# Attention units of two layers: the order of mixed probabilities and maxima on VectorE, two first convolution taps on ScalarE, two taps moved

## The reference

```python
p = jax.nn.softmax(sc, axis=-1)              # causal scores of both components of a head
a = p[:, :, 0] - lam * p[:, :, 1]            # mixed probabilities
o = jnp.einsum('bhqk,bhkv->bhqv', a, vt)
...
u = ga * jax.nn.sigmoid(gb)
u = causal_depthwise_conv(u, dw_conv_w[l], dw_conv_b[l])   # 31 taps and a bias for each channel
u = jax.nn.silu(layer_norm(u, conv_ln_g[l], conv_ln_b[l]))
```

## Time and profile before

| | |
|---|---|
| median of 3 runs | 1059.52 us (1059.42 to 1060.04) |
| profiled execution: time, span | 1060.15 us, 1058.0 us |
| TensorE busy | 1027.0 us (97%) |
| VectorE busy | 831.6 us (79%) |
| ScalarE busy | 525.1 us (50%) |
| attention units, layer 0 | about 396 to 447 us of the span |
| attention units, layer 1 | about 758 to 810 us of the span |

### The profile page before, as it was taken

The page is one execution under the profiler, slowest core; times in us unless marked ns, Lnnn a source line. Parts: engine busy times, 40 slices in busy tenths (PEclk is TensorE's granted clock), DMA queues, the critical chain, the costliest instruction groups (busy, mean ns, idle before and its releaser), DMA issues.

```text
span 1058.0 us, 19244 instructions
## 1 busy us (share of the span) xinstructions
PE 1027.0 (97%) x8174; PEld 983.7 (93%) x8174; DVE 831.6 (79%) x1117; ACT 525.1 (50%) x625; POOL 29.7 (3%) x54
## 2 busy tenths in 40 slices
PE   7999899999999999999999999999999999999998
PEld 6788899999998988989999999999888899999998
DVE  5889599998875999977988886879999676555552
ACT  5564665554435535545544343464455455444441
POOL 5100000000000010000000000000000000000000
PEclk9999999999999999999999999999999999999998
DMA  8576249799892654348599998846442475666551
GB/s 278 176 242 233 103 180 320 275 321 331 315 338 76 201 170 158 120 161 307 190 365 317 323 331 297 289 136 221 142 158 80 155 243 186 193 188 194 178 180 40
DMA packets 137473, 230.37 MB, mean 218 GB/s; under 512 B 7107, under 2 KB 60715, under 8 KB 137389
## 3 DMA queue, kind: packets, MB, share of 16 engines
q1 hardware_dynamic: 135060, 227.05, 62.8%
q10 hardware_dynamic: 921, 1.32, 0.5%
q0 software_dynamic: 1408, 0.79, 0.5%
HBM read 227.29 MB, written 1.06 MB: 216 GB/s over the span
## 4 chain that ended last, share of the span: by engine, by line
PE 69%; DVE 22%; ACT 6%; issue 2%; DMA 1%; SPq 0%; DVEq 0%; ACTq 0%
PE mm L437 66%; DVE lo L1313 7%; DVE cacc L1403 6%; ACT hi L852 1%; DVE ada_acc L1329 1%; DVE sB L1419 1%; DVE qk L1438 1%; DMA swap<-qk 1%; DVE hf L1436 1%; DVE qk L1437 1%; DMA raw<-in_w_in_dram 1%; DVE pB L1848 0%; DVE sA L1419 0%; ACT pB L931 0%; PE pa L544 0%
## 5 line engine op out<-in xcount | busy, mean ns | idle before, releaser
L437 PE MATMUL mm<-act_hi,hi 128*128 128x256 f32 x1760 | 487.7, 281 | 4.4 <-ACT act_hi L920 2.3
L437 PE MATMUL mm<-act_hi,lo 128*128 128x256 f32 x1760 | 483.0, 278 | 0.0
L437 PE MATMUL mm<-act_lo,hi 128*128 128x256 f32 x1760 | 466.0, 278 | 0.0
L1313 DVE TENSOR_TENSOR lo<-raw,hi 128x2048 fp32r<-128x2048 f32 (+1 forms) x159 | 359.5, 2264 | 117.8 <-ACT hi L852 114.8
L852 ACT ACTIVATE hi<-raw 128x2048 fp32r<-128x2048 f32 (+1 forms) x159 | 300.4, 1893 | 227.6 <-PE mm L437 172.7
L437 PEld LDWEIGHTS mm<-act_hi,hi 128*128 128x128 f32 x1760 | 332.2, 189 | 10.4 <-issue 7.2
L437 PEld LDWEIGHTS mm<-act_hi,lo 128*128 128x128 f32 x1760 | 333.5, 189 | 0.3
L437 PEld LDWEIGHTS mm<-act_lo,hi 128*128 128x128 f32 x1760 | 321.3, 189 | 0.0
L437 PE MATMUL mm<-u_hi,hi 128*128 128x256 f32 x608 | 169.3, 278 | 0.0
L437 PE MATMUL mm<-u_lo,hi 128*128 128x256 f32 x608 | 168.7, 278 | 0.0
L437 PE MATMUL mm<-u_hi,lo 128*128 128x256 f32 x608 | 168.7, 277 | 0.0
(11 more groups left out here) (285 smaller groups left out, 880.7 us busy)
## 6 DMA issues: line engine op xcount, KB each, us to landing
ada_raw<-in_ada_w_dram SPq DMA_DIRECT2D x128, 384.0 KB, 5.2
raw<-in_w_ffn_in_dram SPq DMA_DIRECT2D x88, 512.0 KB, 5.2
raw<-in_w_in_dram SPq DMA_DIRECT2D x39, 1024.0 KB, 5.1
raw<-in_w_ffn_out_dram SPq DMA_DIRECT2D x20, 1024.0 KB, 6.0
raw<-in_w_up_dram SPq DMA_DIRECT2D x16, 1024.0 KB, 6.5
raw<-in_w_down_dram SPq DMA_DIRECT2D x16, 1024.0 KB, 7.5
raw<-in_w_out_dram SPq DMA_DIRECT2D x12, 1024.0 KB, 5.9
raw<-in_w_in_dram SPq DMA_DIRECT2D x16, 512.0 KB, 6.2
```

Source lines behind the costliest of these rows:

```text
L437: ins = pe.matmul(o, w[:, kk, fs], a[:, k, :], start=(k == 0 and i == 0 and f % 2 == 0), stop=(ends and i == len(pairs) - 1), skip_group_c ...
L1313: v(dve.tensor_tensor(lo[:, c % RING, 0:nk, :], raw[:, c % RING, 0:nk, :], hi[:, c % RING, 0:nk, :].bitcast(F32), ALU.subtract), "lo_done")
```

## The change

- In units 0, 2 and 4 `probs2(i + 1)` (with the wait for its exponentials) is called ahead of `softmax_max(i + 2)` and `softmax_max(i + 3)`; the odd units 1, 3 and 5 don't call it any more. Unit 7 does as before.
- The first taps of channel tiles 2 and 3 are made by ScalarE: two activations (Identity, with the tap's weight as scale and the bias) on 128x256, ahead of the hi splits of group 2's stage, once VectorE has released `second_gated`. VectorE's generator leaves them out, hands out 122 taps, and waits for `second_begun` at that place.
- Two taps move: `TAPS_AT_IN[6]` goes from 7 to 5, `TAPS_AHEAD[1]` from 0 to 2.

```diff
@@ -41,8 +41,8 @@
 FAR = 3e38
 FAR_EXP = 41.0
 
-TAPS_AT_IN = (5, 8, 8, 8, 8, 0, 7, 1)
-TAPS_AHEAD = (5, 0, 5, 0, 5, 0, 8, 6)
+TAPS_AT_IN = (5, 8, 8, 8, 8, 0, 5, 1)
+TAPS_AHEAD = (5, 2, 5, 0, 5, 0, 8, 6)
 TAPS_BEHIND = (2, 9, 2, 9, 2, 9, 1, 0)
 UNITS = 8
 TAPS = 31
@@ -1153,6 +1153,10 @@
                 for g in (0, 1):
                     steps((l, "in", g))
                     evacuate((l, "in", g), qk2[:, 4 * g:4 * g + 4, :])
+                wait("second_gated")
+                for k in (2, 3):
+                    a(act.activation(cacc[:, k, :], cu[:, k, 0:S], ACT.Identity, scale=convw[:, GT * l + k, 0:1],
+                                     bias=pcols(("convb", l))[:, k:k + 1]), "second_begun")
                 steps((l, "in", 2))
                 evacuate((l, "in", 2), v2[:, :, :])
 
@@ -1396,10 +1400,15 @@
                     w = convw[:, GT * l + k, j:j + 1]
                     src = cu[:, k, j:j + S]
                     name = "conv_done" if j == TAPS - 1 else f"conv_step{k}"
+                    if j == 0 and k == 2:
+                        wait("second_begun", 2)
+                    if j == 0 and k >= 2:
+                        continue
                     if j == 0:
                         v(dve.tensor_scalar(cacc[:, k, :], src, w, pcols(("convb", l))[:, k:k + 1], ALU.mult, ALU.add), name)
                     else:
-                        dve.wait_ge(sem(f"conv_step{k}"), v.n.seen(f"conv_step{k}"))
+                        if j > 1 or k < 2:
+                            dve.wait_ge(sem(f"conv_step{k}"), v.n.seen(f"conv_step{k}"))
                         v(dve.scalar_tensor_tensor(out=cacc[:, k, :], in0=src, scalar=w, in1=cacc[:, k, :], op0=ALU.mult, op1=ALU.add), name)
                     yield
 
@@ -1813,7 +1822,7 @@
                     dve.wait_ge(sem(name), value)
                     k = slice(2 * part, 2 * part + 2)
                     u = cu[:, k, TAPS - 1:]
-                    link(dve.scalar_tensor_tensor(out=u, in0=csq[:, k, :], scalar=1.0, in1=u, op0=ALU.add, op1=ALU.mult))
+                    link(dve.scalar_tensor_tensor(out=u, in0=csq[:, k, :], scalar=1.0, in1=u, op0=ALU.add, op1=ALU.mult), "second_gated" if part else None)
 
                 def taps(count):
                     for _ in range(count):
@@ -1870,11 +1879,13 @@
                 for i in range(UNITS):
                     name, j = todoB(l)[i]
                     taps(TAPS_AHEAD[i])
-                    probs2(i)
+                    if i % 2 == 0 or i + 1 == UNITS:
+                        probs2(i)
                     advance(groups[name][1][j])
                     if i % 2 == 0 and i + 2 < UNITS:
+                        wait("exp_done", 2)
+                        probs2(i + 1)
                         softmax_max(i + 2, sB)
-                        wait("exp_done", 2)
                         softmax_max(i + 3, sB)
                     taps(TAPS_BEHIND[i])
                 heads_normed(slice(0, 2))
```

## The result

The changed kernel took 1063.01 us (median of 7 runs, 1061.18 to 1064.86), the kernel before 1060.04 us beside it (7 runs, 1058.81 to 1062.3). The ratio is 1.0032, with a 95% interval of 1.0019 to 1.0046: **slower by 0.32%**, some 3.4 us (the two medians lie 3.0 us apart). The prediction had 1061.3 us and a range up to 1062.9, so the time lies 0.1 us outside. Of the three outcomes (faster, same, slower) it is the one that had a chance of 0.33.

What follows compares the result with a forecast made beforehand. The prediction took VectorE to pace the changed part up to unit 6's reciprocal, with TensorE beside it. VectorE and what follows -0.44 us, clock +2.2, total +1.76 on the median of 1059.52: 1061.3 us, range 1058.9 to 1062.9.

Steps and rivals of the forecast that it cites:

- VectorE's chain: VectorE up to unit 6's reciprocal, per layer: +0.14 us for the taps, about -0.21 us for the reordering.
- The tail: Last taps after `heads_normed`, 12 becoming 10: sum over channels ready sooner, -0.15 us per layer, bounds 0 and -0.2.
- Hidden, 0.7 us to spare: ScalarE's two first-tap activations, 0.85 us ahead of a hi split, end before VectorE needs that split, costing nothing.
- Where the freed stall goes: TensorE leaves turn 5 about 3.1 us sooner, then idles 2.6 to 3.0 us ahead of turn 7, before `heads_out`.
- the clock's term: TensorE's clock falls to half around `heads_out` after the gathered idle: +1.1 us per layer, 2.2 in all, bounds 0 and 3.4.
- The placing: Low-clock stretch of 3.4 us starts 1.2 us after the idle's end; 2.5 us lie on `heads_out`, losing 1.25 us.
- the second rival: Low-clock stretch lies wholly on `heads_out` in both layers: +2.96 us, 1062.5 us; chance 0.31 of passing its deciding point.
- the sum's +1.76 us: Whole-kernel total: -0.44 us from VectorE and what follows, plus 2.2 us for the fallen clock, both layers.
- the first rival: TensorE's clock stays up in both layers, leaving only -0.44 us: 1059.1 us; chance 0.22.

Runs made afterwards that it cites:

- the run with the late probabilities: Kernel before with three more taps between unit 6's reciprocal and unit 7's probabilities (`TAPS_AHEAD[7]` from 6 to 9), old order; ratio 0.9967 (0.9933 to 1.0000).
- two taps earlier: Changed kernel with the old order on VectorE and two taps fewer ahead of unit 6's reciprocal (`TAPS_AHEAD[6]` from 8 to 6); ratio 0.9987 (0.9957 to 1.0016).
- the taps alone: Changed kernel with the old order on VectorE, keeping first taps on ScalarE and the two moved taps; ratio 0.9993 (0.9953 to 1.0034).

## Why the prediction came out as it did

**VectorE's chain: right.** The reciprocal of unit 6 was to come 0.07 us earlier and came 0.05 earlier. The two parts were seen apart: -0.19 for the reordering (-0.21 in the sum), +0.17 for the taps (+0.14). The lo splits of the place with the new activations didn't move, there was no table load, and turn 1's stall of 2.0 us shrank to 0.72.

**The tail: right in kind, small in size.** Two taps fewer were to give 0.15 us. `heads_out` to the sum went from 7.82 to 7.64, which is 0.18, and from there to the conv branch from 9.30 to 9.20: 0.28 in all.

**"Hidden, 0.7 us to spare": true in the first profile, not in others.** The two activations take 0.98 us, not 0.85, by ScalarE in the changed kernel's own profile: the hi split starts 385.87 - 384.89 behind the first.

```profile
384.89 1.08 ACT L1158 ACTIVATE cacc<-cu,parT,convw 128x256 f32<-128x256 f32 x2
385.87 1.91 ACT L852 ACTIVATE hi<-raw 128x2048 fp32r<-128x2048 f32 x1
```

The cover was taken from one profiled execution, and it depends on when TensorE ends its chunk. In 8 of the 18 layers profiled with them in this place it was used up, and the reciprocal came 0.4 us late. With the two behind the values' copy the wait was gone.

**"Where the freed stall goes": the step that failed.** That the stall is gathered ahead of the last turn, and that the clock then falls on `heads_out`, is what happened. What was wrong is the working between, and the size of the clock's term that came out of it: +1.1 us per layer, measured 1.41 and 1.64. I let the turn of unit 5 start as soon as the probabilities were there, 3.4 us behind the start of the lo split. It starts 4.94 us behind, when the second maxima have freed its bank. TensorE so leaves turn 5 only 1.68 us sooner (66.29 us from g, before 67.97), not 3.1, and the idle time is 1.44 us, not 2.6 to 3.0. From this I would have argued that the clock stays up, for a 1.62 us idle had passed. It fell all the same in 4 of 6 layers, so the sign of the term came out right partly by luck. Two idle times of 1.44 and 1.00 us with 0.6 us of work between them were enough, sometimes. The placing was wrong too. I put the low stretch 1.2 us behind the idle's end, 0.9 ahead of `heads_out`; it begins 1.4 us behind it in layer 0 and 1.9 in layer 1, so 0.5 ahead of `heads_out` and with it. It takes 1.41 and 1.64 us there, more than even the 1.25 of that placing. Both are past the 1.28 at which the second rival decides, so in its own profile the changed kernel did what that rival says: 2.37 us lost in the two layers, less than its 2.96 because the stretch of layer 0 began 0.5 us ahead of `heads_out` (3.05 in both, not 3.4) and because what VectorE and the tail gave back was 0.68, not 0.44. So the sum's +1.76 us is 2.37 by the layers; the rest of the measured 3.4 stays open (below).

The rule of the Trainium skill that the first rival stood on (TensorE: Matmul & The Clock Gate, section "HAM oscillation — how this bites in real kernels"), that only longer gaps are to be feared, would have given 1059.1 us. The traces disagree: with 1.44 and 1.00 us the clock fell in 4 of 6 layers, and with one idle time of 3.03 us in both. But what I held against the rival, that 2.0 us "did not pass", was one case: in the run with the late probabilities 2.02 us did (last section).

**Cause, and what stays open.** Shown: each fall costs the path 1.4 to 1.7 us. It came in 7 of the 12 layers with the idle times that the reordering gathers, and in none of the 16 others; in the 6 layers where they were filled there was none, which at 7 in 12 would come by chance once in some 190 times. Argued only: how often it falls. The changed kernel's excess at the lower level was 4.0 to 5.3 us per execution on the first chip (taking the 8.9 to 10.2 us of before from the others), and 2.8 and 2.3 on the next two. At half speed that costs 2.0 to 2.6, 1.4 and 1.2 us, against 0.66 us gained in both layers together (99.41 to 99.08, where nothing falls). So it should come to +1.3 to +2.0 us on the first chip and +0.5 to +0.7 on the others. The others agree within their wide intervals. The first comparison, 3.4 us with an interval of 2.0 to 4.9, lies above, and what it has beyond 2.0 has no cause that these runs show. Two things could carry it and were not measured by themselves. The lower-level time of before includes stretches behind turn 1, as in the earlier trace rows, that cost the path nothing, so the differences above may be too small a measure of what `heads_out` lost. And the stages run at two paces (last section), which moves an execution by more than the whole change. In the profile, some 0.8 us went between the conv branch's start and the first half of layer 0's output projection (31.58 us instead of 30.78), to the first addition of its result. Some 0.2 of it is a longer wait ahead of that projection, and 0.6 are the same matmuls at the slower pace. That stretch took 30.9 to 32.2 in layer 0 of other kernels, so I don't count it to the change.

**A better version**, by the count of layers, is the one with the first taps behind the copy of the values, two taps earlier and the idle time filled. It starts the conv branch 0.83 us sooner per layer than the kernel before (98.58 against 99.41), 1.7 us in all, and with the old order and no filling it is 0.61 per layer, 1.2 in all. Neither is shown as time: 1.7 us is 0.16%, and the intervals are 0.4% to each side.

## What to carry to other kernels

When a stall in the middle of a stage is removed, ask which dependency at the stage's end has not moved: TensorE arrives there early and idles directly ahead of the work that sets the end, where here a fallen clock cost 1.4 to 1.7 us each time, while behind turn 1 it cost nothing. A step that gets its data sooner must also get its buffer sooner, so look at who frees the bank it writes to. Cover that was read from one execution, here 0.7 us on ScalarE, should be larger than the shift of TensorE between executions before it is priced at nothing.

## What the runs showed of the hardware

The same stage runs at two paces with the granted clock at 1.00 throughout. Two windows within the stages of large projections, changed kernel (columns as above), and then the same windows of the kernel before:

```profile
160.00:300.00 140.00, 140.00 (x1191) 140.00 (x1190) 122.98 (x95) 69.78 (x50) 0.00 (x0) 1.00 0.88 308
530.00:680.00 150.00, 150.00 (x1326) 150.00 (x1325) 133.23 (x110) 66.27 (x53) 0.00 (x0) 1.00 0.96 332
```

```profile
160.00:300.00 140.00, 140.00 (x1238) 140.00 (x1237) 126.49 (x97) 71.58 (x51) 0.00 (x0) 1.00 0.90 319
530.00:680.00 150.00, 150.00 (x1276) 150.00 (x1275) 127.57 (x107) 63.99 (x50) 0.00 (x0) 1.00 0.93 319
```

A matmul takes 140 / 1191 = 0.1175 us in the one and 0.1131 in the other; in the later stage it is the other way round. The places of the gated products bear it out: from layer 0's to layer 1's 357.95 us in the changed kernel, 362.91 before. One pace or the other moves a program by about 5 us for each such stage, more than the whole change; the profiled spans of all these kernels ran from 1052.7 to 1074.4 us, and the two paces may be most of it, which was not measured by itself. What picks the pace is not known.

Second, the clock fell behind idle times of 1.44 and 1.00 us in some layers and not in others of one execution, with the same instructions around them.

The same holds for a single idle time. Turn 1 of the run with the late probabilities, layers 0 and 1, and the windows behind it:

```profile
411.11 0.75 PE L577 MATMUL pv<-cst,pB 128*128 128x128 f32 x3 [2.01 <-DVE pB L1848]
...
766.95 0.55 PE L577 MATMUL pv<-cst,pB 128*128 128x128 f32 x3 [2.02 <-DVE pB L1848]
```

```profile
411.30:414.70 3.40, 3.40 (x18) 3.40 (x18) 3.40 (x5) 2.80 (x10) 0.00 (x0) 0.50 0.30 69
766.90:770.30 3.40, 3.35 (x29) 3.35 (x30) 3.40 (x5) 2.77 (x10) 0.00 (x0) 1.00 0.27 95
770.30:774.00 3.70, 3.70 (x33) 3.53 (x33) 3.70 (x10) 1.28 (x1) 0.00 (x0) 1.00 0.84 277
```

At turn 1 of the five kernels profiled with the old order the clock fell behind 2.01 us (before, layer 0), 2.01 us (late probabilities, layer 0), 2.53 us (the taps alone, layer 0) and 1.84 us (two taps earlier, layer 1). It did not behind 2.02 us, behind 1.84 us twice, nor behind 1.45 to 1.63 us (3 layers). So the length of the idle time alone doesn't tell whether it falls.
